# Attention output read back during the scan, split during the group norm and multiplied between the gates; second norm by logarithm; six slots for the down product

## The reference

```python
h = rmsnorm(x, norm1_g) * (1 + sc1) + sh1
z = h @ w_in                                  # r,k,v | codes | q,k,v of attention | branch gates
y_b = attention(qb, kb, vb)                   # context, or neighbourhood and context
y_a, s_fin = rwkv_branch(r, k, v, xw, xa, xg, s0)     # scan in both directions
#   inside: mu, var over each head of 64; y = (y - mu) * rsqrt(var + GN_EPS) * gn_w + gn_b
#           y = (y + bonus) * (sigmoid(xg) @ gate_up)
mixed = sigmoid(ga) * (y_a @ w_out_a) + sigmoid(gb) * (merge_heads(y_b) @ w_out_b)
x = x + g1 * (mixed @ w_out)
h2 = rmsnorm(x, norm2_g) * (1 + sc2) + sh2
u, gte = split(h2 @ w_ffn_up); u = dwconv3(u, conv_ffn)
x = x + g2 * ((gelu(u) * gte) @ w_ffn_down)   # then the final norm
```

## Time and profile before

| what | value |
|---|---|
| runs before | 2361.28, 2367.15, 2369.21 us; median 2367.15 |
| profiled execution | 2367.85 us, span 2365.8 us |
| TensorE busy | 2184.1 us, 92% (23068 matmuls) |
| VectorE, ScalarE, GpSimd busy | 1446.5, 828.9, 826.3 us (61%, 35%, 35%) |
| mean granted clock of TensorE | 0.973 of full |
| moved | 294.73 MB, mean 125 GB/s |

### The profile page before, as it was taken

One profiled execution on the slowest core, in us unless ns is written; L12 is line 12 of the kernel. 1 busy time (PEld: TensorE's weight loads), 2 busy tenths in 40 slices (PEclk: granted clock), 3 DMA queues, 4 the chain that ended last, 5 costly groups with the idle time before them and its releaser, 6 DMA issues. The chain is left out here.

```text
span 2365.8 us, 53206 instructions
## 1 busy us (share of the span) xinstructions
PE 2184.1 (92%) x23068; PEld 1904.0 (80%) x23068; DVE 1446.5 (61%) x2189; ACT 828.9 (35%) x1379; POOL 826.3 (35%) x459
## 2 busy tenths in 40 slices
PE   5899999999999988899699994999999999998987
PEld 4676776888888878888388874999999999787877
DVE  5867735284676678965656239665656656444456
ACT  5345245334655533333500013322222222222234
POOL 1112111211111122222443442766767674332333
PEclk9899999999999999999899996999999999999999
DMA  8322301224677876764134120121211213543445
GB/s 315 120 84 77 112 11 41 104 80 124 191 188 199 214 216 195 208 192 139 58 113 178 71 107 18 59 87 59 76 70 59 87 59 111 199 147 120 147 153 194
DMA packets 243107, 294.73 MB, mean 125 GB/s; under 512 B 144896, under 2 KB 182656, under 8 KB 241280
## 3 DMA queue, kind: packets, MB, share of 16 engines
q1 hardware_dynamic: 217600, 289.32, 37.2%
q10 hardware_dynamic: 25344, 3.15, 0.9%
HBM read 215.73 MB, written 76.68 MB: 124 GB/s over the span
## 5 line engine op out<-in xcount | busy, mean ns | idle before, releaser
L1069 PE MATMUL PS<-buffer,buffer 128*128 128x320 f32 (+2 forms) x3152 | 1084.0, 344 | 90.1 <-DVE buffer L2725 21.4
L1070 PE MATMUL PS<-buffer,buffer 128*128 128x320 f32 (+2 forms) x3152 | 1069.9, 339 | 0.0
L1071 PE MATMUL PS<-buffer,buffer 128*128 128x320 f32 (+2 forms) x3152 | 1069.1, 339 | 0.0
L1069 PEld LDWEIGHTS PS<-buffer,buffer 128*128 128x128 f32 x3152 | 601.9, 191 | 165.6 <-issue 90.3
L1071 PEld LDWEIGHTS PS<-buffer,buffer 128*128 128x128 f32 x3152 | 601.5, 191 | 52.2
L1070 PEld LDWEIGHTS PS<-buffer,buffer 128*128 128x128 f32 x3152 | 602.9, 191 | 49.8 <-issue 1.0
L2998 POOL TENSOR_TENSOR buffer<-buffer,buffer 128x512 fp32r<-128x512 f32 x154 | 262.7, 1733 | 50.8 <-ACT buffer L2147 46.2
L3018 POOL TENSOR_TENSOR buffer<-buffer,buffer 128x512 fp32r<-128x512 f32 x66 | 117.5, 1782 | 249.4 <-ACT buffer L2215 249.4
L2920 POOL TENSOR_TENSOR buffer<-buffer,buffer 128x1024 fp32r<-128x1024 f32 x28 | 72.1, 2575 | 353.5 <-ACT buffer L1951 353.5
L2147 ACT ACTIVATE buffer<-buffer 128x512 fp32r<-128x512 f32 x110 | 69.1, 632 | 309.6 <-POOL buffer L2992 166.7
L2841 DVE TENSOR_TENSOR buffer<-buffer,buffer 128x512 fp32r<-128x512 f32 x66 | 48.9, 741 | 169.3 <-ACT buffer L2215 169.1
(11 more groups left out here) (254 smaller groups left out, 3027.9 us busy)
## 6 DMA issues: line engine op xcount, KB each, us to landing
buffer<-in_w_down SPq DMA_DIRECT2D x66, 512.0 KB, 3.4
buffer<-in_w_up SPq DMA_DIRECT2D x44, 512.0 KB, 3.9
buffer<-in_w_in SPq DMA_DIRECT2D x42, 512.0 KB, 4.9
ops_kept<-buffer SPq DMA_DIRECT2D x40, 512.0 KB, 5.1
buffer<-ops_kept SPq DMA_DIRECT2D x80, 256.0 KB, 3.3
buffer<-in_w_ada SPq DMA_DIRECT2D x32, 512.0 KB, 4.0
buffer<-rkv_kept SPq DMA_DIRECT2D x120, 128.0 KB, 3.6
fact_kept<-buffer SPq DMA_DIRECT2D x22, 640.0 KB, 2.9
```

The source lines that it names most:

```text
L1069: mm(out, w_hi, x_hi, start=start, stop=False)
L1070: mm(out, w_hi, x_lo, start=False, stop=False)
L1071: return mm(out, w_lo, x_hi, start=False, stop=stop)
```

## The change

1. The read of yb (2560 KB) goes from behind the scan into its turn 14, behind the load of the solved blocks.
2. ScalarE rounds yb's four blocks between the squares and deviations of the group norm and no longer after it; GpSimd, whose program is the same, thus makes their rests earlier.
3. TensorE's order is gate 0, gate 1, first mixing product, gate 2, gate 3, second mixing product; in that last one the loop over the blocks k is the outer one, with a wait for each.
4. The second norm is exp(-0.5 ln(mean square + eps)) on ScalarE; VectorE's three reciprocals are gone. Behind it VectorE makes t3 after t4 and after the rests of t1, t2 and b22; the buffers of s1 and a22 are exchanged.
5. The down product has six slots. The loads of steps 3 to 5 go around the read-back of x1; each load from step 3 on also waits until step j - 3 is rounded. Steps 0 and 1 are rounded ahead of the last gelu and split ahead of the last convolution.

```diff
-        SLOTS = 3
-        s5 = Space(FREE)
+        SLOTS = 6
+        SLOT = 2 * KB * P + 1024
...
+        for at in [FREE, FREE + SLOT, FREE + 2 * SLOT, block_at[11], RING, RING + SLOT]:
+            s5 = Space(at)
...
-        ROUNDS_FIRST = ["a11", "s4", "s2", "a22", "s1", "s3"]
+        ROUNDS_FIRST = ["a11", "s4", "s2", "s1", "s3", "a22"]
...
+                if i == 14:
+                    sp.dma_start(yb4.rearrange("p j t -> p (j t)"), dram["yb_kept"]).then_inc(yb_kept, 16)
...
-            sp.dma_start(yb4.rearrange("p j t -> p (j t)"), dram["yb_kept"]).then_inc(yb_kept, 16)
...
             def load_down(j):
                 if j >= SLOTS:
                     sp.wait_ge(w_used, step_used(j - SLOTS))
+                if j >= 3:
+                    sp.wait_ge(w_round, DOWN_ROUND + j - 2)
+                    sp.wait_ge(fact_rounded, j - 2)
...
             sp.wait_ge(h2_ready, LOW_ROWS["b22"] + 4)
+            sp.wait_ge(h2_scaled, T_AT + 16)
...
-            for j in range(NP):
-                gate(j)
-                if j == NP - 2:
-                    pe.wait_ge(w_split, MIX_TILE + 1)
-                    pe.wait_ge(yc_ready, 3 * NP)
-                    mix_half(0, 0)
-            mix_half(0, 1)
+            gate(0)
+            gate(1)
+            pe.wait_ge(w_split, MIX_TILE + 1)
+            pe.wait_ge(yc_ready, 3 * NP)
+            mix_half(0, 0)
+            gate(2)
+            gate(3)
+            pe.wait_ge(ya_ready, 3 * NP)
+            for k in range(NP):
+                pe.wait_ge(y_split, NP + k + 1)
...
+            act.wait_ge(yb_kept, 32)
+            round_yb(0)
+            round_yb(1)
             for j in range(NP):
+                if j in (1, 2):
+                    round_yb(j + 1)
                 act.wait_ge(yc_ready, 3 * j + 3)
...
-                act.activation(row_factor[:, t0:t0 + m], PS[:, 3 + g, 0:m], ACT.Sqrt, bias=eps_c[:, 0:1], scale=1.0 / D) \
-                    .then_inc(ms_ready, 1)
+                A.step(act.activation(row_factor[:, t0:t0 + m], PS[:, 3 + g, 0:m], ACT.Ln, bias=eps_c[:, 0:1], scale=1.0 / D))
+            A.settle()
+            for g, (t0, m) in enumerate(SEGS):
+                act.activation(row_factor[:, t0:t0 + m], row_factor[:, t0:t0 + m], ACT.Exp, scale=-0.5).then_inc(ms_ready, 1)
...
+            for j in range(2):
+                round_down(j)
             gelu(FB - 1)
...
-                    dve.reciprocal(row_factor[:, a:a + n], row_factor[:, a:a + n]).then_inc(rs_done, 1)
...
+                if f == FB - 1:
+                    for j in range(2):
+                        split_down(j)
                 V.link(ts(u, upad[:, 1:ZP - 1], conv_taps("conv_ffn", f, 1), None, ALU.mult))
...
             for j in range(NSTEP):
-                split_down(j)
+                if j >= 2:
+                    split_down(j)
```

More of the change, by code:

```diff
@@ L1034, in _ @@
             sp.wait_ge(w_used, product(FB - 1, P2 + 1))
-            for j in range(SLOTS):
+            for j in range(3):
                 load_down(j)
@@ L2111, in first @@
                 return isinstance(n, int) and n == 0
-            act.wait_ge(yb_kept, 32)
-            for k in range(NP):
-                act.activation(ybH[:, k, :], yb4[:, k, :], ACT.Copy).then_inc(y_rounded, 1)
             for k in range(NP):
@@ L2175, in _ @@
             act.wait_ge(h2_scaled, T_AT + 4)
-            for name in ("s4", "s2", "a22"):
+            for name in ("s4", "s2", "s1"):
                 round_up(0, name)
             round_t("t1", 4)
-            act.wait_ge(h2_scaled, T_AT + 12)
-            round_up(0, "s1")
             round_t("t2", 8)
@@ L2197, in _, with round_down @@
                         round_up(f + 1, name)
+            def round_down(j):
+                slot, m = j % SLOTS, DOWN[j // FB][1]
+                act.wait_ge(ring_in[j % 3], RING_IN + 32 * (j // 3) + 32)
+                act.activation(down_hi[slot], down_w[slot], ACT.Copy).then_inc(w_round, 1)
+                act.activation(down_fH[slot][:, 0:m], down_f[slot][:, 0:m], ACT.Copy).then_inc(fact_rounded, 1)
+            for j in range(2):
+                round_down(j)
             gelu(FB - 1)
@@ L2761, in _ @@
                     ALU.add, ALU.subtract).then_inc(h2_scaled, 1)
-            for k in range(4):
-                stt(made["t3"][:, k, :], x1[:, 4 + k, HALF:T], shift_step[:, 1, k:k + 1], x1[:, k, HALF:T],
-                    ALU.add, ALU.subtract).then_inc(h2_scaled, 1)
             dve.wait_ge(h2_scaled, T_AT + 8)
+            V.settle()
+            low("t1", None, 2 * KB + 1)
             dve.wait_ge(w_split, split_at(0, "s4"))
```

57 lines of the change are left out of this document (35 added, 22 removed).

## The result

| | before | after |
|---|---|---|
| median of the runs of this comparison (4 and 4) | 2368.18 us | 2330.26 us (2329.10 to 2330.69) |
| span of the profiled execution | 2365.8 us | 2328.6 us |
| mean granted clock of TensorE | 0.973 | 0.979 |

The ratio is 0.9847, 95% interval 0.9832 to 0.9861: 38 us faster. The forecast was 2318 with a range of 2306 to 2335. The time is inside the range and 12 us above the forecast. Most terms held in sign, mechanism and size; the scan's had the wrong mechanism, and that of the start of the down product the wrong size.

A forecast was written before the change was run, and what follows sets the result against it. TensorE, busy nearly throughout, was taken as the bound, so other engines count only where it waits. Terms -2.0 + 11.5 + 4.8 + 3.9 + 10.3 + 9.9 + 10.5 = 48.9 us gave 2318 us, range 2306 to 2335.

The forecast's parts named there:

- The scan: Turn 14: the attention output's read delays the next turn's loads behind it in SyncE's queue; a loss of 2.0 us.
- start of the down product: Early splits of the first two operands gain 9.4 us, then a new stall at step 4; net gain 3.9 us.
- Group norm and first mixing block: Early rounding and splitting, and the second product ordered by block, end that product earlier; gain 11.5 us.
- four meetings: VectorE instructions meeting GpSimd's splits in the group norm: 2.0 us a meeting by the row, possibly 3.59 by the skill.
- Second norm: Square root and reciprocals go: 5.5 us up to the sums, reordered work behind them not reduced; gain 4.8 us.
- The changes of column: Down product: six slots remove TensorE's two waits, each with 1.95 us of half clock; gains 10.3 and 9.9 us.
- The last column: End of the down product: with six slots loads run ahead and gaps from late loads close; gain 10.5 us.
- my first rival: Six slots help less, the down start stalls for the whole read-back, the norm gives 2 us: 2332 us, chance 0.20.
- The second rival: Everything overlaps better: no scan loss, no stall at step 4, 15 us in the mixing stage: 2307 us, chance 0.17.

The follow-up runs named there:

- The kernel without a stall: The changed kernel with the loads of down steps 4 and 5 ahead of the residual and final gain read back: 2322.2 us.
- the kernel with both edits: The changed kernel with the attention output read behind all loads of the scan, and down loads 4 and 5 ahead of the residual: 2313.5 us.

## Why the prediction came out as it did

**The scan: wrong, by 6.3 us, the largest miss, and past the far end of 5 us that I gave it.** The step that failed is the one that priced the read from what stands behind it in SyncE's queue alone, and that put "many small store packets of ScalarE's queue" at 5 us at most, as something that slows the read. It was the reverse: the read slowed the issuing of the stores, on ScalarE, with the turn's copy behind it. In seven kernels with the whole read at turn 14 that turn took 17.0 to 19.9 us, 6.4 to 9.3 too many. The mechanism that I did price is real, 2.2 us in turn 16 of the kernel with the read one turn later. I had expected the longer turn to be 15 and 1 to 4 us longer; both were off. The earlier trace rows show only SyncE's issues and one eviction; the trace that they come from had what was needed, the eight issues in turn 14 with the copy 0.1 us behind them, and turns 6 and 12 made longer by such stores. I looked for who waits for SyncE's loads and not for who else issues DMAs in that turn.

**Group norm and first mixing block: right, 11.1 against 11.5.** The delay of the chain was 3.8, not 3.0; the rest of the chain came to the tenth (product 37.7 us behind the first mean, as I had 1151 against 1113.3; two last blocks 16.6 us). One argument was idle: the place of the first product between the gates is worth nothing. What the part gives comes from the early rounding and splitting and from the order by block. By the Trainium skill (SBUF — State Buffer, Who interferes with whom) I had put the loss at 9.0 if four meetings cost 3.59 us each. The chain had only two, of 3.76 and 2.75 us in place of 1.55, and the second moved it by no more than 0.3; no meeting up to the second product took VectorE over 2.6 us more (4.11 for 1.55). So the row was the better guide, for the price and for the count.

**Second norm: right, 4.5 against 4.8,** with both table loads there. The 5.5 us up to the sums came as 5.6, the reordered work cost 0.8 to 1.1 (I had 0.7). That this came so near is in part luck: I had put VectorE at 28.8 us up to the third factor's split, and it took 31.0; the wait for the rounding came as put, the 2.0 us on the sums were not in it, and the earlier third product gave some back.

**Start of the down product: the place right, the size wrong.** Both early splits removed the pause at the start, and the stall came at step 4 as forecast. It was 5.1 us and 3.2 of half clock where I had 3.8 and 1.7. The kernel without a stall gives the two changes of column: 267.2 - 239.3 = 27.9, of which the old start had 9.3; after keeps 8.3 of these, so the term was 1.1 and not 3.9. In seven other kernels with the same order of loads the stage took 245.2 to 246.9, which makes it 1.7 to 3.4, with stalls of 4.1 to 4.7 us: the trace of after is the worst of eight here, and part of this miss is scatter of the DMAs. From the first rounding at 2023.99 to the last split's end took 3.45 us, as put (3.5); it is the landing that came 1.4 us later after the start of the product than I had it, and the 5 MB ahead of it took 19.2 us and not the 16.5 of the earlier trace rows.

**The changes of column: right,** 18.6 us in this stage (18.2 forecast). **The last column: right,** 12.1 (12.4), bound by TensorE alone. The denser stream of transfers that it was priced with did not come: 219 GB/s, not 270, against 213 before.

So of the 12 us between forecast and time, 6.3 are the scan, 2.8 the stall at step 4, 1.9 the scatter ahead of turn 14, and the rest small misses. None of these made up for another of weight (the changes of column gave 0.4 more than forecast); the time is inside because the range had room for them. It lies beside that of my first rival, 2332, but not by its mechanism. That had the last column give 3 us besides the pause ahead of it and the norm 2, and they gave 10.2 and 4.5; only its third part, nothing gained at the start of the down product, came near the 1.1 us of the trace, and it gave the scan no more than I did. The second rival's 2307 would have needed the stall and the read away: the kernel with both edits took 2313.5.

## What to carry to other kernels

Before a large transfer is put into a steady loop, look in that turn for every engine that issues DMAs itself, and at what stands behind these instructions in its queue; a computing engine that issues its own stores does no work behind them while an issue is held up, as here beside a read of 2.5 MB. One load that is needed soon belongs ahead of a bulk read that is needed late: two lines moved gave 8 us here. Of a reordering whose gain is argued from one product being ready earlier, ask what ends the stage: here it was a split behind all of them, and the order lost about 1 us.

## What the runs showed of the hardware

- Eight DMA issues of ScalarE, 0.66 us each at a DMA share of 0.4, took 11.5 us in all beside a read of 2560 KB (single ones up to 3.9 us, 5.4 in another run), and 6.5 us beside one of 1280 KB.
- Behind these pauses TensorE's granted clock fell to the lower level (1.2 GHz): 0.55 mean over 7.6 us in turn 14 of the scan, where the kernel before had 1.00 throughout, and 0.52 over 6.5 us behind the stall at step 4. The first lost 2.3 us behind a wait of 5.8, the second 3.2 behind one of 5.1.
- A logarithm and an exponential in turn had a table load of 1.28 us before each, here too.
- A split of VectorE in the down stage (128x512, two inputs) took 1.75 us beside GpSimd's (1.77 us from 2025.13) and 0.68 without it.
